# Gate tiles of a second block's mixing stage: pairs by seven half-size block products in place of eight

## The reference

```python
for l in range(DEPTH):                                  # 2 layers
    h = rmsnorm(x, norm_mix_g[l])
    proj = h @ w_in[l]                                  # 1024 x 7328; the last 3072 columns are gate logits
    ...                                                 # y_a, y_b, y_c: three attention branches, 512 x 512 each
    branches = jnp.stack([y_a, y_b, y_c], axis=2)
    up = jnp.einsum('bsnw,nwd->bsnd', branches, w_branch[l])
    gates = jax.nn.sigmoid(gate_logits.reshape(B, S, N_BRANCH, D_MODEL))
    x = x + jnp.einsum('bsnd,bsnd->bsd', gates, up) @ w_out[l]
    h = rmsnorm(x, norm_mlp_g[l])
    x = x + jnp.square(jax.nn.relu(h @ w_up[l])) @ w_down[l]
```

## Time and profile before

| | |
|---|---|
| median of 3 runs | 3602.91 us (3602.59 to 3605.31) |
| profiled execution, first to last instruction | 3601.9 us |
| instructions | 48925 |
| HBM read, written | 330.49 MB, 2.10 MB |
| gate stages: first sigmoid in layer 0, last in layer 1 | 2079.1 us, 3198.4 us |

### The profile page before, as it was taken

How to read it: one execution, slowest core, us unless ns; L and a number is a source line. 1 busy time by engine, 2 the same in 40 slices (tenths; PEclk the granted TensorE clock), 3 DMA queues, 4 the chain that set the end, 5 groups by cost and what they waited for, 6 DMA issues and landing times.

```text
span 3601.9 us, 48925 instructions
## 1 busy us (share of the span) xinstructions
PE 3528.8 (98%) x19524; PEld 3022.3 (84%) x19524; DVE 2178.0 (60%) x3405; ACT 1637.7 (45%) x2902; POOL 621.5 (17%) x457
## 2 busy tenths in 40 slices
PE   8999999999999999999999999999999999999999
PEld 6898889999989777888767778889986777888998
DVE  4838797666665465445656443677756554348775
ACT  4246545444452563233457332444445744245444
POOL 0100043222210000000100001444410000125442
PEclk8999999999999999999999999999999999999999
DMA  7610332222234232233211323232221132332322
GB/s 264 204 43 1 117 124 65 71 71 71 62 148 163 71 119 83 92 102 98 83 53 54 104 87 98 95 104 96 101 93 55 47 100 82 97 116 86 104 99 77
DMA packets 127524, 342.06 MB, mean 95 GB/s; under 512 B 12992, under 2 KB 45632, under 8 KB 126784
## 3 DMA queue, kind: packets, MB, share of 16 engines
q1 hardware_dynamic: 118800, 306.42, 25.8%
q10 hardware_dynamic: 8496, 32.51, 2.6%
HBM read 330.49 MB, written 2.10 MB: 92 GB/s over the span
## 4 chain that ended last, share of the span: by engine, by line
PE 81%; DVE 7%; ACT 3%; issue 1%; POOL 1%; DVEq 0%; ACTq 0%; POOLq 0%
PE ps L897 34%; PE ps L1281 15%; PE ps L1800 10%; PE ps L1333 5%; PE ps L952 5%; PE ps L933 2%; PE ps L1645 1%; DVE wlo L2953 1%; PE ps L1456 1%; PE ps L1444 1%; PE ps L1435 1%; DVE prod L3027 1%; PE ps L1165 1%; PE ps L1138 1%; ACT whi L1858 1%
## 5 line engine op out<-in xcount | busy, mean ns | idle before, releaser
L2953 DVE TENSOR_TENSOR wlo<-raw,whi 128x1024 fp32r<-128x1024 f32 (+3 forms) x583 | 634.2, 1094 | 513.0 <-ACT whi L1858 512.9
L1858 ACT ACTIVATE whi<-raw 128x1024 fp32r<-128x1024 f32 (+3 forms) x583 | 498.3, 857 | 625.3 <-PE ps L897 182.7
L897 PE MATMUL ps<-bh,whi 128*128 128x512 f32 x768 | 307.0, 400 | 0.0
L897 PE MATMUL ps<-bh,wlo 128*128 128x512 f32 x768 | 299.2, 390 | 0.5 <-DVE wlo L2953 0.5
L897 PE MATMUL ps<-bl,whi 128*128 128x512 f32 x768 | 299.2, 390 | 0.0
L897 PE MATMUL ps<-ah,wlo 128*128 128x384 f32 (+1 forms) x768 | 247.1, 362 | 1.2 <-DVE wlo L2953 1.2
L897 PE MATMUL ps<-ah,whi 128*128 128x384 f32 (+1 forms) x768 | 247.6, 363 | 0.0
L897 PE MATMUL ps<-al,whi 128*128 128x384 f32 (+1 forms) x768 | 246.8, 362 | 0.0
L4092 POOL TENSOR_TENSOR sq<-sq,sq 128x512 f32<-128x512 f32 x50 | 75.9, 1518 | 809.4 <-ACT sq L1913 809.3
L1800 PE MATMUL ps<-uh,whi 128*128 128x512 f32 x504 | 196.2, 389 | 0.0
L1800 PE MATMUL ps<-ul,whi 128*128 128x512 f32 x504 | 196.2, 389 | 0.0
(11 more groups left out here) (537 smaller groups left out, 9061.3 us busy)
## 6 DMA issues: line engine op xcount, KB each, us to landing
raw<-weights_d SPq DMA_DIRECT2D x401, 512.0 KB, 3.5
aw<-ada_d ACTq DMA_DIRECT2D x56, 512.0 KB, 4.2
aw<-ada_d SPq DMA_DIRECT2D x40, 512.0 KB, 7.8
raw<-weights_d SPq DMA_DIRECT2D x80, 256.0 KB, 2.6
x<-weights_d SPq DMA_DIRECT2D x30, 512.0 KB, 4.5
raw<-weights_d SPq DMA_DIRECT2D x44, 192.0 KB, 2.3
x<-nab_d SPq DMA_DIRECT2D x24, 256.0 KB, 2.7
x<-x_t_d SPq DMA_DIRECT2D x4, 1024.0 KB, 5.5
```

The costliest lines, as they stand in the source:

```text
L897: m = e.matmul(p[:, 0:n], tiles(w, i)[:, k, :], xs[:, x0 + k, c0:c0 + n], start=pi == 0 and k == 0 and ti == 0, stop=i == job and k == kt ...
L1858: e.activation(like(flat(WHI, key), src), src, ACT.Copy).then_inc(q.did("hi", key))
L2953: e.tensor_tensor(lo, src, hi.bitcast(F32), ALU.subtract).then_inc(q.did("lo", key))
```

## The change

The gate tiles are put in one list, m = 0 to 23. The first four are made as before, with branch tiles 0 and 1. The other twenty are made as ten pairs by seven products each. In pair n the tiles are m = 4 + 2n and m + 1; PE makes products 1, 2, 6, 5, 7, then the branch tile m - 2, product 4, branch tile m - 1, product 3. So branch tiles come one pair after their gates, and branch tiles 22 and 23 after the last pair.

Two kinds of sums are new. Before the first pair VectorE makes scaled copies of x (`gb`, two for each j of 4), GpSimd four sums of their halves for each j (`gt_sums`), ScalarE and VectorE the high and low parts of these (`gt_high`, `gt_low`). For each pair GpSimd makes four sums of weights (`gate_sum`), one pair ahead. The copies for j = 2, 3 lie in buffers which retention's last tile uses, and wait for its low part (`rol`). The scale's row is copied by GpSimd before retention (`RSC`).

The products of a pair share three banks. The bank of products 1, 6, 7, 4 is read between them: ScalarE copies its partial result into `G` after products 1, 6 and 7 (`g_snap`), and the next product of that bank waits for the copy. VectorE adds the other banks' results to the copies (`g_join`), and ScalarE takes the sigmoids.

The sum over branches is kept for all eight tiles in `MF`, and its high and low parts are made only after product 7 of the last pair (`m_high`, `m_low`), because `MH` and `ML` take the room of the sums. The load of the up projection's first odd weights waits for that product too; before, it waited for the second branch.

```diff
+GPAIRS = 10
+FIRST_GATE = 4
+LAST_GATES = GPAIRS - 1
...
+    def gates(l):
...
+        for m in range(FIRST_GATE):
+            S("w_in_2", (l,), 0, 8, cols(m), ((0, 2, 1, 2)[m],))
+            if m < 2:
+                branch(m, (1, 0)[m], 2)
+        for n in range(GPAIRS):
+            m = FIRST_GATE + 2 * n
+            even, odd = [raw_only("w_in_2", (l,), 0, 8, cols(m + b)) for b in range(2)]
+            gpair_of[l, n] = even, odd
+            unit(n, 1, "raw", even, 0, 512)
+            unit(n, 2, "raw", even, 512, 512)
+            unit(n, 6, "gsum", 2, l, n)
+            unit(n, 5, "gsum", 1, l, n)
+            unit(n, 7, "gsum", 3, l, n)
+            branch(m - 2, 6, 1)
+            unit(n, 4, "raw", odd, 512, 512)
+            branch(m - 1, 7, 1)
+            unit(n, 3, "gsum", 4, l, n)
+        branch(22, 6, 1)
+        branch(23, 7, 1)
...
+            if i == even:
+                return [("lo", ("g", l, n, 1)), ("lo", ("g", l, n, 2)), ("gsum", 4, l, n)]
+            if i == odd:
+                return [("gsum", 3, l, n), ("lo", ("g", l, n, 4))]
...
+            for n in range(GPAIRS):
+                for _ in range(2):
+                    chunk("w_in_2")
+                a, b, d = gate_banks(n)
+                made = lambda m: (lambda k: [("gtl", l, m, k)]) if n == 0 else None
+                bank(a, ("gc21", l, n))
+                seven(("g", l, n, 1), a, B11, True, False)
+                bank(b, ("gc11", l, n))
+                seven(("g", l, n, 2), b, B21, True, True)
+                seven(("g", l, n, 6), a, T2, False, False, ("gs1", l, n), ready=made(2))
+                bank(d, ("gc12", l, n))
+                seven(("g", l, n, 5), d, T1, True, False, ready=made(1))
+                seven(("g", l, n, 7), a, T3, False, False, ("gs2", l, n), ready=made(3))
+                branch(FIRST_GATE + 2 * n - 2)
+                seven(("g", l, n, 4), a, T4, False, True, ("gs3", l, n), ready=made(4))
+                branch(FIRST_GATE + 2 * n - 1)
+                seven(("g", l, n, 3), d, B22, False, True, ("gc22", l, n))
...
+            for m in range(FIRST_GATE):
+                next(last_, None)
+                i = chunk("w_in_2")
+                if m >= 2:
+                    for j in (2 * m - 4, 2 * m - 3):
+                        for t in (2, 1, 3):
+                            gt_high(t, j)
+                other_table("sigmoid")
...
+            for n in range(GPAIRS):
...
+                rounded(("g", l, n, 1))
+                g_snap(n, 1)
+                if n == 0:
+                    for j in range(4):
+                        gt_high(4, j)
+                rounded(("g", l, n, 2))
+                rounded(("g", l, n, 6))
+                g_snap(n, 2)
...
+            def gb(j):
+                for t, k in ((GB0[j], j), (GB1[j], 4 + j)):
+                    q.wait_ge(("rsc", l), ("rpv", l, 3, 2), *([("rol", l, 3), ("gt", l, 1, j - 2)] if j >= 2 else []))
+                    e.scalar_tensor_tensor(t, lat(X, k), col("norm_mix", 8 * l + k), RSC, ALU.mult, ALU.mult
+                                           ).then_inc(q.did("gb", l, k))
...
+            def m_low(ct):
+                q.wait_ge(("mh", l, ct))
+                e.tensor_tensor(ML[:, ct, :], MF[:, ct, :], MH[:, ct, :].bitcast(F32), ALU.subtract).then_inc(q.did("ml", l, ct))
...
+            gt_sums(0)
+            gt_sums(1)
+            added(1)
+            gt_sums(2)
+            gt_sums(3)
+            for s_ in range(1, 5):
+                gate_sum(0, s_)
+            for n in range(GPAIRS):
+                more = n < LAST_GATES
+                if more:
+                    gate_sum(n + 1, 1)
+                    gate_sum(n + 1, 2)
+                added(FIRST_GATE + 2 * n - 2)
+                if more:
+                    gate_sum(n + 1, 3)
+                added(FIRST_GATE + 2 * n - 1)
+                if more:
+                    gate_sum(n + 1, 4)
...
-                    q.wait_ge(*(raw_free(odds[n - 2]) if n % (UPAIRS - FIRST_UP) >= 2 else [("sbv", plan[i][1][0], 3, 2)]))
+                    q.wait_ge(*(raw_free(odds[n - 2]) if n % (UPAIRS - FIRST_UP) >= 2
+                                else [("mm", ("g", plan[i][1][0], LAST_GATES, 7))]))
```

More of the change, by code:

```diff
@@ new lines, in g_sigmoid @@
+            def g_sigmoid(n, h, t, *ready):
+                other_table("sigmoid")
+                q.wait_ge(*ready)
+                e.activation(gate_tile(n, h)[:, t], gate_tile(n, h)[:, t], ACT.Sigmoid).then_inc(q.did("gsg", l, n, h))
+            for n in range(GPAIRS):
+                for _ in range(2):
+                    next(count)
+                final = n == LAST_GATES
+                rounded(("g", l, n, 1))
[6 more added lines that the diff above has]
+                g_snap(n, 2)
+                rounded(("g", l, n, 5))
+                rounded(("g", l, n, 7))
+                g_snap(n, 3)
+                chunk("w_branch_2")
+                g_sigmoid(n, 1, U_SECOND, ("gc22", l, n))
+                rounded(("g", l, n, 4))
+                if final:
+                    m_high(0)
+                    m_high(1)
+                q.wait_ge(("mm", ("g", l, n, 4)), ("gused", l, FIRST_GATE + 2 * n - 3))
+                e.activation(gate_tile(n, 1)[:, U_FIRST], PS[gate_banks(n)[0]][:, 0:256], ACT.Sigmoid
+                             ).then_inc(q.did("gc21", l, n))
+                q.note("gsig", l, FIRST_GATE + 2 * n + 1)
+                chunk("w_branch_2")
+                rounded(("g", l, n, 3))
+                if final:
+                    m_high(2)
+                    m_high(3)
+                g_sigmoid(n, 0, slice(0, TL), ("gc11", l, n), ("gc12", l, n))
+                q.note("gsig", l, FIRST_GATE + 2 * n)
@@ L2786, in u_high @@
+            chunk("w_branch_2")
+            for ct in (4, 5, 6):
+                m_high(ct)
+            chunk("w_branch_2")
+            m_high(7)
             def u_high(k):
@@ new lines, in dve_program @@
+            for n in range(GPAIRS):
+                for _ in range(2):
+                    next(count)
+                final = n == LAST_GATES
+                rounded(("g", l, n, 1))
+                rounded(("g", l, n, 2))
+                g_join("gc11", n, 2, 1, 0, U_FIRST, "gs1")
+                if n == 0:
+                    for j in range(4):
+                        gt_low(4, j)
+                rounded(("g", l, n, 6))
+                rounded(("g", l, n, 5))
+                rounded(("g", l, n, 7))
+                g_join("gc22", n, 5, 2, 1, U_SECOND, "gs3")
+                gated(FIRST_GATE + 2 * n - 2)
+                rounded(("g", l, n, 4))
+                if final:
+                    m_low(0)
+                    m_low(1)
+                gated(FIRST_GATE + 2 * n - 1)
+                rounded(("g", l, n, 3))
+                if final:
+                    m_low(2)
+                    m_low(3)
+                g_join("gc12", n, 3, 2, 0, U_SECOND, "gs2")
@@ L3941, in u_low @@
+            for ct in (4, 5):
+                m_low(ct)
+            gated(22)
+            m_low(6)
+            gated(23)
+            m_low(7)
             def u_low(k):
@@ L4197, in pool_program, with added @@
             q.note(f"end_ret{l}", "pool")
-            for ct in range(8):
-                for n in range(1, 3):
-                    m = 3 * ct + n
+            def added(m):
+                if m % 3:
                     q.wait_ge(("gprod", l, m), ("gused", l, m - 1))
-                    e.tensor_tensor(ACC[ct % 2], ACC[ct % 2], G[m % 2], ALU.add).then_inc(q.did("gused", l, m))
-                if ct == 0:
-                    q.note(f"end_tail{l}", "pool")
+                    e.tensor_tensor(MF[:, m // 3, :], MF[:, m // 3, :], G[m % 4], ALU.add).then_inc(q.did("gused", l, m))
@@ L4205, in up_sum @@
+            added(22)
+            added(23)
             def up_sum(n, s_):
```

182 lines of the change are left out of this document (125 added, 57 removed).

## The result

The changed kernel took 3630.05 us (median of 4 runs, 3629.54 to 3630.86), the kernel before 3602.76 on the same chip: a ratio of 1.0075, 95% interval 1.0063 to 1.0087, or 27.3 us slower. The forecast was 9.6 us slower, so the sign was right and the size was not. The profiled execution's span is 3627.5 us, 25.6 above the span before.

The account below looks back on a forecast made before the run. TensorE's matmuls were taken to bound the stage, busy 122.00 of 122 us. Terms -16.1 + 20.6 + 3.3 + 1.2 + 0.6 = +9.6 us gave 3612.5 us, range 3598 to 3623.

Parts of the forecast that it names:

- Fewer products: Gate pairs: 84 matmuls of 256 columns replace 48 of 512, saving 0.80 us a pair, 16.1 us in twenty pairs.
- The first pair: Before product 6 in each layer: PE waits 10.3 us for sums and ScalarE's snapshot, 20.6 us in all.
- The clock: After each layer's wait before product 6: granted clock falls to 0.50, costing 3.3 us in two layers (0 to 5).
- The tight chain: Before product 7, twelve later pairs: addition, weight sum 4, branch tile load, rounding, snapshot; 0.1 us each, 1.2 in all.
- rival (c): Steady pairs: slower GpSimd operations (1.72 us) make twelve pairs wait 0.65 us each, 7.8 in all, 3619.1 us; chance 11%.
- All fit, so these cost nothing: Later pairs: VectorE's, ScalarE's and GpSimd's work each fits in a pair's 15.5 us, so no cost.
- The sentence on the load: Later pairs: the next pair's tiles wait for product 4's rounding, some 3.5 us in, and have 12 us to land.
- The end of the stage: Before w_out: VectorE may be a little behind with a rounding, 0.3 us a layer, 0.6 in all (0 to 2).
- The 1.0 us outside the span: Old kernel's three-run median stood 1.0 us above its profiled execution's span; taken as unchanged in the forecast time.
- what I named as making me wrong: Gate stage: longest wait under 7 us, its end on a weight rounding instead of the snapshot, or gaps in every pair.

Follow-up runs that it names:

- the final version: The two edits together, plus VectorE making the last gated product before a w_out low part and the fourth gate tile's low part before later scaled copies: 3590.09 us.
- the first experiment: Changed kernel with GpSimd making weight sum 4 right behind sum 3, ahead of the previous pair's addition: 3624.9 us, ratio 1.0061.
- the two edits together: Changed kernel with weight sum 4, snapshots moved earlier, even tile's sigmoid later, plus six regular gate tiles and nine pairs: 3596.47 us, ratio 0.9979.
- six regular tiles: Changed kernel with six gate and four branch tiles made the regular way first, then nine pairs: 3613.3 us, ratio 1.0027.
- two reorderings: Changed kernel, separately: first pair's sums, parts and snapshot reordered, 3631.16 us; branch tiles 2 and 3 made ahead of the first pair, 3632.4 us.

## Why the prediction was off

**Fewer products: right.** The steps stayed at 0.1200 and 0.2267 us, and the final version keeps 13.9 of 14.4 us. In the pairs, at the granted clock of 1.00, steps of 256-column matmuls longer than 0.120 stand only at the stops (0.22 for the step behind one). The rule cited against it (the Trainium skill, "TensorE: Matmul & The Clock Gate", section "Back-to-back issue gap") gives 131 ns at 512 columns, where the trace has 0.2267 us; the measurement decides.

**The first pair: right, by its own steps.** Forecast 10.3 us, measured 10.30 start to start in both layers, ended by the snapshot as said. GpSimd's sums for j = 2 and ScalarE's queue (timeline after, layer 0):

```profile
2102.42 1.12 POOL L4408 TENSOR_TENSOR x<-gb,gb 128x256 f32<-128x256 f32 x1 [1.95 <-DVE gb L4069]
...
2111.21 1.26 POOL L4426 TENSOR_TENSOR sq<-sq,raw 128x512 f32<-128x512 f32 x1
...
2112.50 1.15 ACT L1930 ACTIVATE whi<-sq 128x512 fp32r<-128x512 f32 x2 [10.83 <-POOL sq L4426]
...
2116.91 0.36 ACT L2874 ACTIVATE g<-ps 128x256 f32<-128x256 f32 x1
```

The operand sums took 7.5 us (2102.42 to 2109.87) where 8.5 was forecast from the earlier trace rows, the scaled copies 4.1 where 2.9 was from the earlier trace rows: errors of opposite sign, so that the sum agrees to the tenth is luck. From weight sum 2 to the end of the snapshot it is 4.8 us, forecast 5.0.

**The clock: right in kind, 4.3 for 3.3.** The same wait of 10.14 us was followed by 27 slow steps in one layer and 16 in the other.

**The tight chain: this step failed.** It was placed rightly, on twelve pairs, and sized at 0.1 us each, with 0.4 as the upper end; it cost 1.03 each, 12.3 us. That is the place that rival (c) named, at more than its price of 0.65. In the chain rows above the two GpSimd operations took 2.95 us, as forecast (2.9). The load took 3.00 in place of 2.6 (2.4 to 3.1 from sum to rounding in the twelve). The rest is the start: the gated product could begin 0.16 us behind the branch tile's last matmul, I wrote, which took VectorE to be free. That fails in half of the twelve. In the six long stops (1.26 to 1.75 us with the step behind) two low parts stood in front of it in VectorE's order, and it began 1.2 to 1.9 us after PE had left the branch tile. In the six short ones (0.35 to 0.66) it began 0.2 to 0.5 us after, and the links behind it add the rest. One of each, layer 0; PE left the branch tiles at 2195.99 and 2213.09:

```profile
2194.64 2.80 DVE L3087 TENSOR_TENSOR wlo<-sq,whi 128x512 fp32r<-128x512 f32 x2 [1.25 <-ACT whi L1930]
2197.37 0.68 DVE L4061 TENSOR_TENSOR g<-ps,g 128x512 f32<-128x512 f32 x1
...
2211.24 1.71 DVE L3087 TENSOR_TENSOR wlo<-sq,whi 128x512 fp32r<-128x512 f32 x2 [1.26 <-ACT whi L1930]
2213.29 0.69 DVE L4061 TENSOR_TENSOR g<-ps,g 128x512 f32<-128x512 f32 x1 [0.34 <-PE ps L945]
```

From the gated product's start to product 7 it is 7.1 to 7.7 us in all twelve, where the terms of the forecast make 7.1. The 0.10 us in the step behind each stop was in no term either. Rival (c) had its price from 1.72 us for each GpSimd operation, and that isn't what opened the chain.

**"All fit, so these cost nothing": this failed too.** I compared each engine's work with the 15.5 us of a pair: VectorE 9.7, ScalarE 8.2, GpSimd 7.9 to 10.3. The windows after show about that (VectorE 106.58 and GpSimd 71.55 of 162 us, 10.7 and 7.2 a pair if they are counted as ten). The work does fit; the loop through four engines and a load, 16.49 us in the first experiment, does not. The stops before product 6, for which I had nothing, cost 3.4 us in the changed kernel and 9.9 and 13.4 once the other chain was cut. The sentence on the load ("have 12 us to land") looked at the matmuls that use the tiles and not at the weight sums, which need both tiles sooner and hand the delay on.

**VectorE beside GpSimd.** Through the first pair the operand sums took 7.5 us, hardly more than twice the 3.5 of the earlier trace rows. It was VectorE that lost time beside them: a low part of 256 columns took 0.95 us there and 0.41 with GpSimd idle (timeline after, layer 0):

```profile
2104.01 0.95 DVE L4078 TENSOR_TENSOR gt2l<-gt2f,gt2h 128x256 fp32r<-128x256 f32 x1
...
2115.84 0.41 DVE L4078 TENSOR_TENSOR gt2l<-gt2f,gt2h 128x256 fp32r<-128x256 f32 x1
```

By the Trainium skill, "SBUF — State Buffer", section "Who interferes with whom", I had the sums and VectorE's work add to 10.6 us, and the total 4.2 us higher. That did not come: PE waited for the sums, and those were hardly held up. In the later pairs, where I did not apply that section, the rows bear it out in kind: two low parts took 2.80 us beside GpSimd's sums, and, in the two edits together, with GpSimd idle:

```profile
2121.44 1.28 DVE L3092 TENSOR_TENSOR wlo<-sq,whi 128x512 fp32r<-128x512 f32 x2
```

**The end of the stage:** 0.7 us a layer where 0.3 was forecast. The last product began at 2287.74, 1.1 us after its branch tile allowed, behind a low part of `w_out`'s weights, one of M and the product before; from there to the last low part of M it was 4.05 us for 3.45. What each is worth in this kernel was not run; with six regular tiles a low part of the same kind was the stop.

**The 1.0 us outside the span** compared a median with one execution's span. In the later runs an execution takes 1.8 to 2.3 us more than its own span, whichever the kernel, so it had next to no part in the difference.

Of what I named as making me wrong, one came true in the main: gaps in 16 of the 18 later pairs.

## What to carry to other kernels

Busy shares say whether work fits, not whether it arrives. When a stage is software-pipelined, write down the loop from one step to the next (a slot freed, a load, sums, roundings, a copy, the slot again) and compare its length with the step; a loop one microsecond too long stopped TensorE in nearly every step here, though no engine but TensorE was busy throughout. Cut it where an in-order queue holds a short, urgent instruction (a snapshot, a sum that frees a slot) behind one that nobody waits for yet. A start-up wait was better covered here with more ready work than shuffled: two reorderings only spread it, and two more regular tiles removed it, for the 0.8 us a layer that one pair saves and two stops that further orders took away.

## What the runs showed of the hardware

VectorE and GpSimd slow each other in both directions, by more than I had counted. VectorE's two low parts went from 1.28 to 2.80 us beside GpSimd. The other way round, in the two edits together, an operand sum of 256 columns took 3.67 us beside six short low parts in a row and a long one behind them, against 0.74 for the one behind it:

```profile
2104.09 3.67 POOL L4415 TENSOR_TENSOR gt2f<-x,gb 128x256 f32<-128x256 f32 x1
2107.84 0.74 POOL L4417 TENSOR_TENSOR gb<-gb,gt2f 128x256 f32<-128x256 f32 x1
```

Second, the granted clock stayed at 1.00 through the short stops of the later pairs in the changed kernel, layer 0 (the window from 2126 us above), but with six regular tiles it fell once more behind a stop of 1.99 us, start to start, at 2196.22, in these 13 us (columns as in the earlier trace rows):

```profile
2190.00:2203.00 13.00, 11.08 (x66) 10.00 (x65) 6.39 (x10) 5.70 (x12) 5.98 (x5) 0.87 0.39 122
```

A stop of 2.19 us in layer 1 of the same execution, at 3128.81, had no such stretch behind it:

```profile
3125.00:3138.00 13.00, 10.97 (x70) 9.78 (x70) 6.98 (x11) 5.26 (x11) 4.17 (x3) 1.00 0.37 122
```

So a stop in the middle of a stage can cost more than itself, and the length of the stop alone does not tell when.
